# Hybrid attention block on one core: the last sixteen keys share the meta queries' step, and each head has four key tiles

## What is computed

```python
def attend(qb, qpos, kk, vv, kpos, qdec=None, kdec=None):
    s = jnp.einsum('bqhd,bkhd->bhqk', qb, kk) * scale
    if qdec is not None:                      # FOX: decay added to the scores
        s = s + qdec - kdec
    s = jnp.where(kpos[None, :] <= qpos[:, None], s, -jnp.inf)
    p = jax.nn.softmax(s, axis=-1)
    return jnp.einsum('bhqk,bkhd->bqhd', p, vv)
...
# FOX, MLA: 8 heads each, causal over all 528 positions
# SWA: 8 query heads on 2 key heads, a window of 128, the meta keys and a sink
meta = attend(q[:, :M], pos[:M], k[:, :M], v[:, :M], pos[:M])       # M = 16
```

## Time and profile before

| | us |
|---|---|
| median of 3 runs | 1981.65 |
| lowest and highest | 1978.85 and 1982.34 |
| span of the profiled execution | 1979.4 |
| PE busy in it | 1914.7 (97%) |
| weight load of PE busy | 1817.1 (92%) |
| DVE busy | 1159.0 (59%) |
| POOL busy | 1025.5 (52%) |
| ACT busy | 766.2 (39%) |

### The profile page before, as it was taken

One profiled execution on the slowest core, in us unless ns is written; L12 is line 12 of the kernel. 1 busy time (PEld: TensorE's weight loads), 2 busy tenths in 40 slices (PEclk: granted clock), 3 DMA queues, 4 the chain that ended last, 5 costly groups with the idle time before them and its releaser, 6 DMA issues.

```text
span 1979.4 us, 36478 instructions
## 1 busy us (share of the span) xinstructions
PE 1914.7 (97%) x14396; PEld 1817.1 (92%) x14396; DVE 1159.0 (59%) x2121; ACT 766.2 (39%) x1514; POOL 1025.5 (52%) x1306
## 2 busy tenths in 40 slices
PE   7899999999999999999998999999999999999999
PEld 7889998888999999999997899988889999999887
DVE  7665476787465666552256654767874655665411
ACT  5455666655223222220044556666553232222100
POOL 7655454544364444544477455544443645445553
PEclk9999999999999999999999999999999999999999
DMA  4212121211232322332332121112112423323332
GB/s 149 75 44 65 54 65 44 63 45 55 65 129 85 97 86 86 97 93 93 93 109 76 43 65 54 63 46 65 45 53 65 141 86 97 97 86 96 96 97 96
DMA packets 44802, 156.30 MB, mean 79 GB/s; under 512 B 5012, under 2 KB 5268, under 8 KB 44504
## 3 DMA queue, kind: packets, MB, share of 16 engines
q1 hardware_dynamic: 44488, 153.75, 24.7%
q10 hardware_dynamic: 144, 0.22, 0.0%
HBM read 149.63 MB, written 4.26 MB: 78 GB/s over the span
## 4 chain that ended last, share of the span: by engine, by line
PE 77%; DVE 12%; ACT 4%; issue 3%; POOL 2%; DMA 1%; SPq 0%; DVEq 0%; ACTq 0%; POOLq 0%
PE ps L1357 20%; PE ps L1360 19%; PE ps L1362 19%; PE ps L1588 5%; PE ps L1372 2%; PE ps L1368 2%; PE ps L1371 2%; PE ps L1376 2%; DVE osum L1993 1%; DVE rstd L1691 1%; PE ps L1540 1%; PE ps L1501 1%; POOL wl L817 1%; DVE ps L1962 1%; DVE square L1686 1%
## 5 line engine op out<-in xcount | busy, mean ns | idle before, releaser
L817 POOL TENSOR_TENSOR wl<-raw,wh 128x256 fp32r<-128x256 f32 x1076 | 798.7, 773 | 746.5 <-DVE wh L1670 739.9
L1357 PE MATMUL ps<-xh,wh 128*128 128x264 f32 (+1 forms) x2880 | 810.7, 303 | 12.5 <-DVE wl L1750 9.4
L1360 PE MATMUL ps<-xl,wh 128*128 128x264 f32 (+1 forms) x2880 | 764.3, 286 | 0.0
L1362 PE MATMUL ps<-xh,wl 128*128 128x264 f32 (+1 forms) x2880 | 585.4, 285 | 0.0
L1357 PEld LDWEIGHTS ps<-xh,wh 128*128 128x128 f32 x2880 | 546.7, 190 | 31.1 <-issue 18.3
L1360 PEld LDWEIGHTS ps<-xl,wh 128*128 128x128 f32 x2880 | 547.4, 190 | 17.0 <-issue 8.9
L1362 PEld LDWEIGHTS ps<-xh,wl 128*128 128x128 f32 x2880 | 451.2, 190 | 0.0
L1670 DVE CAST wh<-raw 128x1024 fp32r<-128x1024 f32 x270 | 206.6, 765 | 176.0 <-PE ps L1357 89.1
L1588 PE MATMUL ps<-pt,vx 128*128 128x512 f32 (+7 forms) x480 | 157.8, 409 | 3.9 <-ACT pt L1274 2.3
L1985 DVE TENSOR_TENSOR ps<-ps,cst 128x128 f32<-128x128 f32 (+6 forms) x240 | 74.8, 313 | 145.3 <-PE ps L1546 111.0
L1274 ACT ACTIVATE pt<-ps 128x256 f32<-128x256 f32 (+5 forms) x224 | 78.5, 363 | 112.5 <-DVE ps L1985 111.2
(11 more groups left out here) (194 smaller groups left out, 3440.9 us busy)
## 6 DMA issues: line engine op xcount, KB each, us to landing
raw<-weights SPq DMA_DIRECT2D x270, 512.0 KB, 3.5
h<-tokens SPq DMA_DIRECT2D x4, 528.0 KB, 6.9
h<-tokens SPq DMA_DIRECT2D x8, 264.0 KB, 6.0
residual<-h SPq DMA_DIRECT2D x8, 264.0 KB, 5.0
h<-residual SPq DMA_DIRECT2D x8, 264.0 KB, 5.9
out<-h SPq DMA_DIRECT2D x8, 256.0 KB, 4.7
cst<-constants SPq DMA_DIRECT2D x1, 1048.0 KB
extra<-positions SPq DMA_DIRECT2D x18, 4.1 KB
```

The lines of the kernel that those rows point to most:

```text
L817: ins = nc.gpsimd.tensor_tensor(wl[c % SPLIT][:, part], raw[:, c % RAW, part], wh[c % SPLIT][:, part].bitcast(F32), ALU.subtract)
L1357: a = nc.tensor.matmul(out, a_hi, x_hi[:, sl], start=first, stop=False)
L1360: nc.tensor.matmul(out, a_hi, x_lo[:, sl], start=False, stop=False)
L1362: ins = nc.tensor.matmul(out, a_lo, x_hi[:, sl], start=False, stop=last)
```

## The change

Each head keeps four key tiles (`KT` = 4) in ST and PV; the fifth, of 17 keys, goes. Its scores are made in STM, beside the meta queries': each head there has two groups of 17 keys by 18 queries, the first keys with the first 18 queries and the last 17 keys with the last 18 queries, in columns 0 to 17 and 18 to 35. One mask on DVE covers both groups; ACT puts the first group's exponentials into rows 0 to 16 of `ptm` and the second's into rows 32 to 48, where `ptm` is block-diagonal. The fifth place of `vx` now holds the first 17 values in rows 0 to 16 and the last 17 in rows 32 to 48, so that one product per head (PVM, 36 columns) gives both. The part for the last 18 queries is put behind column 528 of `oraw` and `osum`, and two new additions on DVE, ahead of the first `recip`, add it to the last 18 columns. `PV_LAG` goes from 2 to 3, so PV of the last tile and O stand at the block where they stood. Two copies of 17 rows are added in each VT. The rotation table `cs` moves out of the constants into slot 3 of the gate buffers and is loaded by DMAs of its own, one in each layer.

```diff
-PV_LAG = 2
+PV_LAG = 3
...
-            for t in range(5):
+            for t in range(KT):
                 i = b + ST_HEAD * e + t
                 put(i, 4, *place(("ST", j, e, t)))
                 put(i + PV_LAG, 5, "PV", j, e, t)
-            put(b + ST_HEAD * e + 4 + PV_LAG + 1, 2, "O", j, e)
+            put(b + ST_HEAD * e + KT - 1 + PV_LAG + 1, 2, "O", j, e)
...
                             if s[0] == "STM":
-                                k0, nk = 0 if br == SWA else 1, META + 1
-                                out, q = bank[0:nk, 32 * e:32 * e + META], slice(0, META)
+                                c0 = 0 if br == SWA else 1
+                                pieces = [(bank[0:ENDS_K, HD * e + a:HD * e + a + ENDS_Q], slice(k0, k0 + ENDS_K),
+                                           slice(q0, q0 + ENDS_Q))
+                                          for a, k0, q0 in ((0, c0, 0), (ENDS_Q, c0 + SEQ, T - ENDS_Q))]
...
-                            ins = nc.scalar.activation(ptm[0:nk, :, :], src[:, :, 0:META], ACT.Exp)
+                            nc.scalar.activation(ptm[0:ENDS_K, :, 0:ENDS_Q], src[:, :, 0:ENDS_Q], ACT.Exp)
+                        ins = nc.scalar.activation(ptm[TAIL:TAIL + ENDS_K, :, ENDS_Q:2 * ENDS_Q],
+                                                   src[:, :, ENDS_Q:2 * ENDS_Q], ACT.Exp)
                         ins.then_inc(meta_probs_ready.sem, meta_probs_ready.tick((l, j)))
...
-                            ins = nc.tensor.matmul(bank[:, 32 * e:32 * e + META],
-                                                   vx[:, v % 2, 0, e * HD:e * HD + P], ptm[:, e, :],
+                            ins = nc.tensor.matmul(bank[:, HD * e:HD * e + 2 * ENDS_Q],
+                                                   vx[:, v % 2, KT, e * HD:e * HD + P], ptm[:, e, :],
                                                    start=True, stop=True)
...
-                                ins = copy(dst[:, 0:4, 2 * e, :], src[:, 0:4, c, :])
+                                copy(dst[0:ENDS_K, KT, 2 * e, :], src[0:ENDS_K, 0, c, :])
+                                ins = copy(dst[:, 0:KT, 2 * e, :], src[:, 0:KT, c, :])
...
+                            for o in (osum, oraw):
+                                ins = nc.vector.tensor_tensor(o[:, T - ENDS_Q:T], o[:, T - ENDS_Q:T], o[:, T:T + ENDS_Q],
+                                                              ALU.add)
+                            step(ins, l, "ends", j)
...
+            sp.dma_start(cs, CST[:, CC_CS:CC_STORED]).then_inc(s_cs, 16)
...
+                if l + 1 < DEPTH:
+                    sp.wait_ge(gate_used.sem, gate_used.at(l, "sum", MLA, 3))
+                    sp.dma_start(cs, CST[:, CC_CS:CC_STORED]).then_inc(s_cs, 16)
```

More of the change, by code:

```diff
@@ L28 @@
 PAIRS = HEADS // 2
+KT = SEQ // P
 MAX_PLACE = (None, 0, 2, 1)
@@ L105, in constants @@
 def constants():
-    c = np.zeros((P, CC_ALL), np.float32)
+    c = np.zeros((P, CC_STORED), np.float32)
     i = np.arange(P)[:, None]
@@ L128, in constants @@
     dist = q - (i - 1)
-    c[:, CC_T0:CC_ALL] = np.where((i <= META) | ((dist >= 0) & (dist < P)), 0.0, NEG)
+    c[:, CC_T0:CC_ENDS] = np.where((i <= META) | ((dist >= 0) & (dist < P)), 0.0, NEG)
+    for window in range(2):
+        for g in range(2):
+            key = i + (SEQ if g else 0) - window
+            query = np.arange(ENDS_Q)[None, :] + (T - ENDS_Q if g else 0)
+            at = CC_ENDS + (window * 2 + g) * ENDS_Q
+            c[:, at:at + ENDS_Q] = np.where(key <= query, 0.0, NEG)
     def factor(n, extra=1.0):
@@ L475, in build @@
     nma = sb("nma", [P, 2, 1])
-    ptm = sb("ptm", [P, 2, META])
+    ptm = sb("ptm", [P, 2, 2 * ENDS_Q])
     epsb = sb("epsb", [P, 1])
@@ L658, in build, with two_groups @@
     last_stat = prior
+    def two_groups(row, by, n):
+        return bass.AP(row.tensor, row.offset, [row.ap[0], [by, 2], [1, n]])
     def rows_of(br, e):
@@ L884, in _ @@
                         settled()
-                        nc.gpsimd.memset(vx[0:META + 1, :, 4, HD:2 * HD], 1.0)
+                        for n, (part, value) in enumerate(((vx[0:ENDS_K, :, KT, HD:2 * HD], 1.0),
+                                                           (vx[TAIL:TAIL + ENDS_K, :, KT, HD:2 * HD], 1.0),
+                                                           (vt[:, TK - 1:TK], 0.0))):
+                            nc.gpsimd.memset(part, value).then_inc(pool_step.sem, pool_step.tick((l, "ends", n)))
+                            began["last"] = (pool_step.sem, pool_step.n)
+                            settled()
                         nc.gpsimd.memset(vt[:, 0:1], 0.0).then_inc(pool_step.sem, pool_step.tick((l, "values")))
@@ L1283, in _ @@
                             own, other = slice(e * HD, (e + 1) * HD), slice((1 - e) * HD, (2 - e) * HD)
-                            copy(oraw[own, 0:META], bank[own, 32 * e:32 * e + META])
-                            ins = copy(osum[own, 0:META], bank[other, 32 * e:32 * e + META])
+                            parts = [bank[r, HD * e:HD * e + 2 * ENDS_Q].rearrange("p (g c) -> p g c", c=ENDS_Q)
+                                     for r in (own, other)]
+                            copy(two_groups(oraw[own, 0:ENDS_Q], T, ENDS_Q), parts[0])
+                            ins = copy(two_groups(osum[own, 0:ENDS_Q], T, ENDS_Q), parts[1])
                         ins.then_inc(meta_heads_copied.sem, meta_heads_copied.tick((l, j)))
@@ L1534, in _ @@
                             else:
                                 k0, nk, q0, nq = key_tile(br, s[3])
-                                out, q = bank[0:nk, 0:nq], slice(q0, q0 + nq)
-                            keys = slice(k0, k0 + nk)
-                            rows = rows_of(br, e)[1]
-                            low = slice(0, MQ) if br == MLA else slice(0, P)
-                            nc.tensor.matmul(out, xk[rows, i, e, keys], xq[rows, i, e, q], start=True, stop=False)
-                            if br == MLA:
-                                nc.tensor.matmul(out, xk[low, i, e, keys], yq[low, i, e, q], start=False, stop=False)
-                                ins = nc.tensor.matmul(out, yk[low, i, e, keys], xq[low, i, e, q], start=False,
-                                                       stop=True)
-                            else:
-                                ins = nc.tensor.matmul(out, yk[low, i, e, keys], yq[low, i, e, q], start=False,
-                                                       stop=True)
+                                pieces = [(bank[0:nk, 0:nq], slice(k0, k0 + nk), slice(q0, q0 + nq))]
@@ new lines, in _ @@
+                            for out, keys, q in pieces:
+                                nc.tensor.matmul(out, xk[rows, i, e, keys], xq[rows, i, e, q], start=True, stop=False)
+                                if br == MLA:
+                                    nc.tensor.matmul(out, xk[low, i, e, keys], yq[low, i, e, q], start=False, stop=False)
+                                    ins = nc.tensor.matmul(out, yk[low, i, e, keys], xq[low, i, e, q], start=False,
+                                                           stop=True)
+                                else:
+                                    ins = nc.tensor.matmul(out, yk[low, i, e, keys], yq[low, i, e, q], start=False,
+                                                           stop=True)
@@ L1966, in _ @@
                         br, p = JOBS[j]
-                        nk = META + 1
-                        a = CC_TRI + (1 if br == SWA else 0)
-                        sc = banks[place["bank"]][0:nk, 0:64].rearrange("p (e c) -> p e c", c=32)[:, :, 0:META]
-                        mask = cst[0:nk, a:a + META].rearrange("p (e c) -> p e c", e=1).broadcast_to([nk, 2, META])
+                        nk = ENDS_K
+                        a = CC_ENDS + (2 * ENDS_Q if br == SWA else 0)
+                        sc = banks[place["bank"]][0:nk, 0:2 * HD].rearrange("p (e c) -> p e c", c=HD)[:, :, 0:2 * ENDS_Q]
+                        mask = cst[0:nk, a:a + 2 * ENDS_Q].rearrange("p (e c) -> p e c", e=1).broadcast_to(
+                            [nk, 2, 2 * ENDS_Q])
                         dve.wait_ge(meta_scores.sem, meta_scores.at(l, j))
```

87 lines of the change are left out of this document (45 added, 42 removed).

## The result

| | before | after |
|---|---|---|
| median of 4 runs, us | 1981.99 | 1995.30 |
| lowest and highest | 1978.85 to 1982.88 | 1994.33 to 1996.77 |
| span of the profiled execution | 1979.4 | 1992.5 |
| PE busy in it | 1914.7 | 1905.5 |
| span less PE busy | 64.7 | 87.0 |

The ratio is 1.0066 with an interval of 1.0052 to 1.0081. The forecast was 1974.0 us with a range up to 1981.5: wrong in sign, and outside the range.

A forecast was written before the change was run, and what follows sets the result against it. PE was taken as the only full engine, 1914.7 of 1979.4 us busy. The terms -10.6 + 1.3 + 1.7 - 1.5 + 1.5 = -7.6 us took the median from 1981.65 to 1974.0 us, range 1965.0 to 1981.5.

The forecast's parts named there:

- The additions: DVE ahead of the reciprocals: each pair holds DVE 0.3 us, felt at some waits; +1.5 us, bounds 0 and 3.
- PV one block later: PV products on PE: their waits for exponentials mostly go; -1.5 us, bounds 0 and -3.8.
- Next is the bank: ST 0 3 takes ST 0 0's bank; in `pt`, exponentials have three blocks of cover, 2.2 us.
- Removed products: PE: 48 products of 16 or 18 columns go at 0.22 us each; -10.6 us.
- Where PE's saving is lost: PE waiting on DVE's queue: six removed products, all in MLA jobs, give back 1.3 us; bounds 0 and 3.5.
- The longer STM: ST 0 2 waits for `ptm` behind ACT's added exponential: 0.21 us at eight places; +1.7 us, bounds 0 and 6.
- ACT, DMA, the rotation table: Added ACT exponentials and copies, and the table's own transfers: nothing; at most 1 us for ACT, 0.5 for DMA and POOL.
- Rival 1, the clock: PE's clock falls behind longer waits at four further places, 3.4 us each; slower, 1987.7 us; chance 0.10.
- Rival 2: DVE sets the attention's pace, two thirds of PE's 10.6 us become waiting; no change, 1979.7 us; chance 0.18.

The follow-up runs named there:

- e1: Changed kernel without the two additions (leaves out adding the last keys' part), PV_LAG still 3; 1983.6 us.
- e3: Changed kernel with PV_LAG back at 2 and without the two additions (leaves out adding the last keys' part); 1975.8 us.
- e2: Changed kernel with PV_LAG back at 2, additions kept on DVE; 1991.6 us.
- e4: Kernel before plus two DVE multiplications by ones on 128x18, two SBUF inputs each, ahead of the first reciprocal; 1994.9 us.
- e9: Kernel before plus two reciprocals of 128x18 ahead of the first reciprocal, the last reciprocal shorter by their columns; 1989.6 us.
- e14: Changed kernel with the additions on POOL and four `pt` buffers in place of three, PV_LAG 3; 1982.7 us.
- e15: Changed kernel with the additions on POOL, four `pt` buffers and PV_LAG 2; 1977.1 us.
- e8: Changed kernel with PV_LAG 2 and the two additions on POOL, at the first reciprocal's block; 1975.4 us.
- e7: Changed kernel with PV_LAG 2 and both additions in one DVE instruction ahead of the last reciprocal; 1979.6 us.

## Why the prediction was wrong, point by point

The miss is 13.3 + 7.6 = 20.9 us. By the medians of the runs: the additions cost 11.7 (changed kernel less e1) instead of 1.5, so +10.2; PV one block later costs 7.8 (e1 less e3) instead of gaining 1.5, so +9.3; all the rest brings 6.1 us (e3 less before) instead of 7.6, so +1.5. Taken in the other order, over e2, the additions have 15.7 and PV 3.7, so the division between the two holds to some 4 us only.

- **The additions: the failed step.** I wrote "a pair holds DVE for 0.3 us" from the earlier trace rows, took 0.3 us at a few waits, and so had 1.5 us with bounds of 0 and 3. Two things were wrong. First, the wait for POOL was missing: the trace has no POOL instruction at 24.36 us, so the row shows the duration without its condition. The wait doubles the pair's mean and takes the first instruction up to 1.3 us, and a queue with PE behind it passes that on. By e4 and e9 it is worth about 5 us. Second, even a pair that waits for nobody costs 8.1 us (e9), in more places than I had counted and with the clock behind them. The own time was nearly right (0.28 us at job 8 in e4, 0.38 for e9's reciprocals). The trace of before had the hint for the first point, a DVE instruction that takes 1.23 us instead of a median of 0.71 while POOL works:

```profile
406.69 1.43 POOL L817 TENSOR_TENSOR wl<-raw,wh 128x256 fp32r<-128x256 f32 x2
...
407.44 1.23 DVE L1688 SCALAR_TENSOR_TENSOR square<-ssum,square 128x528 f32<-128x528 f32 x1
...
L1688 DVE SCALAR_TENSOR_TENSOR square<-ssum,square x28: 647/709/1231, 28.6 to 1610.4; 128x528 f32<-128x528 f32 x28
```

- **PV one block later: right about PV, wrong about the sum.** PV's waits did go. The second step that failed is "Next is the bank", where I looked only for late exponentials and took three blocks of cover as enough. Other waits of PE came instead, 8.4 us for 3.4 (e14 beside e15). What was missing: a product on PE is also work that lets ACT catch up. Bounds of 0 and -3.8 excluded the sign that came.
- **Removed products: right.** From the seventh to the fifteenth block of a job both heads' products go. In the first SWA job of layer 0 these blocks begin at 239.44 and 250.12 us before, and in e3 at 236.38 and 246.61: 10.68 less 10.23 is 0.45 us for two products. In e8, 19 of the 24 jobs show 0.35 to 0.48 here, the 2 x 0.22 of my price.
- **Where PE's saving is lost: too small.** Behind those blocks, up to the next job, e8 gives back 2.7 us in layer 0 and 2.9 in layer 1, 5.6 in all, where I had 1.3 with a bound of 3.5. Jobs 1, 2, 5, 6, 8 and 9 (counted from 0) give back 0.17 to 0.48 each; I had counted MLA jobs alone.
- **The longer STM:** 1.9 to 2.3 us of waiting on `ptm` beside 1.7, and 1.5 us at PVM that I had at nothing.
- **The rest as a whole: near, partly by luck.** e8 also gains 4.6 us between the jobs' first and seventh blocks, for which I had no term; 1.5 of them lie where the kernel before runs 6.8 us at 1.2 GHz behind 300.4 us and e8 only 3.4. Why these blocks gain is otherwise open. Without it e8 would not have come within 2 us of the forecast.
- **ACT, DMA, the rotation table: right.** The start of the first block and the whole feed-forward part stand where they stood: the difference between the kernels does not change from 570 to 1004 us. On ACT's copies of the values PE waits 0.4 us, once.
- **Rival 1, the clock,** had the sign but not the cause. The changed kernel's profiled run has 27.3 us at 1.2 GHz beside 20.5, so 3.4 us of the 13.3 are clock there; by the mean over the runs, 0.992 beside 0.995, I estimate 6. **Rival 2** described the kind of loss, not its size: it let waits eat the saving, never more.

## What to carry to other kernels

Price an added DVE instruction by what POOL runs at that moment, not by the instruction's shortest row, when both work in SBUF. In this kernel POOL is busy half the time, and 18 columns waited up to 1.15 us for a POOL instruction. But look at the queue behind it as well: a pair of 0.38 us that never waited still cost 8 us, since PE waits for that queue in many places. If an addition isn't needed at once, give it to the other engine (e8) or put it where little is queued behind it (e7). Before moving a product away from where it stands, ask who is late at that place: work that needs nothing from the late engine is what covers it.
